# Both FFN up projections as seven half-size products: two weight sums per layer in HBM, two on VectorE

## The reference, cut to what matters

```python
# first layer
h = rms_norm(x, norm2_g)                       # 512 x 1024
gate, val = split(h @ w_up, 2)                 # w_up: 1024 x 5632; each result 512 x 2816
gate = silu(causal_depthwise_conv(gate, ffn_dw_w, ffn_dw_b))   # 3 taps over tokens
x = x + (gate * val) @ w_down                  # w_down: 2816 x 1024
# second layer: the same with w_gate_2 and w_up_2 (1024 x 2816 each), w_down_2, and a final norm
```

## Time and profile before

| | us |
|---|---|
| median of three executions | 1204.06 |
| profiled execution, its own time | 1203.35 |
| span of the profile | 1201.5 |
| TensorE busy | 1169.1 (97%) |
| VectorE busy | 688.9 (57%) |
| ScalarE busy | 560.1 (47%) |
| GpSimd busy | 531.6 (44%) |

### The profile page before, as it was taken

The page is one execution under the profiler, slowest core; times in us unless marked ns, Lnnn a source line. Parts: engine busy times, 40 slices in busy tenths (PEclk is TensorE's granted clock), DMA queues, the critical chain, the costliest instruction groups (busy, mean ns, idle before and its releaser), DMA issues.

```text
span 1201.5 us, 17233 instructions
## 1 busy us (share of the span) xinstructions
PE 1169.1 (97%) x6948; PEld 976.3 (81%) x6948; DVE 688.9 (57%) x979; ACT 560.1 (47%) x881; POOL 531.6 (44%) x288
## 2 busy tenths in 40 slices
PE   7999999999999998999999999999899999999997
PEld 6877768788888886888877767778799999998886
DVE  5999973343332334444574577865956666674444
ACT  6356575333232323232445565655566665652323
POOL 3540033655545454445684220008445555564443
PEclk9999999999999998999989999999999999999999
DMA  5422021268978968867823120213255555642321
GB/s 181 140 78 96 4 70 35 71 231 226 236 242 207 243 234 209 201 243 203 207 57 113 64 71 28 80 37 106 70 169 182 182 187 178 191 162 83 105 89 70
DMA packets 115672, 167.75 MB, mean 140 GB/s; under 512 B 3363, under 2 KB 95882, under 8 KB 115594
## 3 DMA queue, kind: packets, MB, share of 16 engines
q1 hardware_dynamic: 102634, 120.26, 30.2%
q0 software_dynamic: 12800, 46.14, 16.0%
q10 hardware_dynamic: 160, 0.26, 0.1%
HBM read 164.29 MB, written 48.23 MB: 177 GB/s over the span
## 4 chain that ended last, share of the span: by engine, by line
PE 88%; DVE 5%; ACT 3%; issue 1%; POOL 1%; DMA 1%; POOLq 0%; ACTq 0%; DVEq 0%; SPq 0%
PE ps L2294 16%; PE ps L1960 13%; PE ps L1962 13%; PE ps L1961 13%; PE ps L2351 10%; PE ps L2355 10%; PE ps L2049 4%; PE ps L2539 3%; PE ps L2095 1%; DVE act_t L1508 1%; PE ps L2491 1%; PE ps L2080 1%; ACT w_hi L744 1%; PE ps L2410 1%; PE ps L2446 1%
## 5 line engine op out<-in xcount | busy, mean ns | idle before, releaser
L610 POOL TENSOR_TENSOR w_lo<-w_raw,w_hi 128x1024 fp32r<-128x1024 f32 x176 | 445.2, 2532 | 518.2 <-ACT w_hi L744 517.3
L744 ACT ACTIVATE w_hi<-w_raw 128x1024 fp32r<-128x1024 f32 x220 | 231.7, 1055 | 278.7 <-PE ps L1962 84.5
L1960 PE MATMUL ps<-h_hi,w_hi 128*128 128x512 f32 x656 | 261.7, 399 | 3.0 <-DVE h_lo L1347 2.1
L1961 PE MATMUL ps<-h_lo,w_hi 128*128 128x512 f32 x656 | 255.7, 390 | 0.0
L1962 PE MATMUL ps<-h_hi,w_lo 128*128 128x512 f32 x656 | 255.7, 390 | 0.0
L1558 DVE TENSOR_TENSOR tt<-act_t,tt 128x512 fp32r<-128x512 f32 x44 | 97.8, 2232 | 117.1 <-ACT tt L971 117.1
L1960 PEld LDWEIGHTS ps<-h_hi,w_hi 128*128 128x128 f32 x656 | 123.1, 188 | 36.3 <-issue 7.5
L1962 PEld LDWEIGHTS ps<-h_hi,w_lo 128*128 128x128 f32 x656 | 123.1, 188 | 26.2
L1961 PEld LDWEIGHTS ps<-h_lo,w_hi 128*128 128x128 f32 x656 | 123.2, 188 | 24.5 <-issue 0.5
L1565 DVE TENSOR_TENSOR ps<-ps,rbs 128x512 f32<-128x512 f32 x88 | 61.5, 698 | 120.2 <-PE ps L1962 118.9
L2294 PE MATMUL ps<-tt,w_hi 128*128 128x256 f32 x640 | 116.2, 283 | 0.0
(11 more groups left out here) (331 smaller groups left out, 1949.3 us busy)
## 6 DMA issues: line engine op xcount, KB each, us to landing
w_raw<-in_w_up SPq DMA_DIRECT2D x23, 1024.0 KB, 6.9
w_raw<-in_w_down SPq DMA_DIRECT2D x22, 1024.0 KB, 4.9
w_raw<-blocks SPq DMA_DIRECT2D x40, 512.0 KB, 3.6
w_raw<-in_w_in SPq DMA_DIRECT2D x19, 1024.0 KB, 5.1
blocks<-in_w_up POOLq DMA_DIRECT2D x12, 1408.0 KB, 10.5
blocks<-in_w_gate POOLq DMA_DIRECT2D x12, 1408.0 KB, 6.3
blocks<-blocks POOLq DMA_DIRECT2D x8, 1408.0 KB, 10.4
w_raw<-in_w_gate SPq DMA_DIRECT2D x20, 512.0 KB, 3.6
```

The source lines that it names most:

```text
L610: pool.tensor_tensor(unit_view(w_lo, at, flat), unit_raw(at, flat), unit_view(w_hi, at, flat).bitcast(F32), ALU.subtract).then_inc(s_lo, 1)
L744: act.activation(unit_view(w_hi, at, flat), unit_raw(at, flat), ACT.Copy).then_inc(s_hi, 1)
L1960: pe.matmul(ps[:, bank, :], whi, hi, start=first, stop=False, skip_group_check=True)
L1961: pe.matmul(ps[:, bank, :], whi, lo, start=False, stop=False, skip_group_check=True)
```

## The change

`NC` becomes `(1, 1)`: in both layers the first group stays plain and ten are blocks of seven products. Per layer only two weight sums are made in HBM, with 16 DMAs of the same size: S1 (unit of product 0) and S2 (unit of product 6). The first layer's 16 are issued by GpSimd during the first layer's in projection and attention (four among its units, eight in a row after unit 15, four in the out projection), the second layer's 16 during the first layer's up and down projection, one per block. The two other sums (units of products 3 and 4) are made by VectorE: S1 + A11 and then (S1 + A11) + A12, from the blocks of products 0, 1 and 2 that are loaded anyway, into a new buffer `sum_raw` of two units. So a block loads five units, not seven. A load may only overwrite a block after VectorE has used it (`s_sum`).

In the first block of a layer the products run in the order 1, 2, 0, 3, 4, 5, 6. The activations times the norm's gain are now written out once (`xg`, eight ScalarE instructions of 128x512 per layer), and the four activation sums are one VectorE instruction each of 128x1024, all after the norm's `spread`. The low parts of the activation sums move into the first group and first block. In the last block the first two `split_hi` and `split_lo` come earlier, and the down projection starts with banks 0 to 5 of its first two units before banks 6 and 7. The first four units of the down projection are loaded one by one. The cut diff:

```diff
-NC = (11, 1)
+NC = (1, 1)
 def on_vector(u):
-    return block_of(u) is not None and block_of(u)[1] in (1, 3, 5)
+    at = block_of(u)
+    return at is not None and at[1] in (1, 3, 5) and at not in ((0, 1), (NS[0], 1))
+SUMS_AFTER = {u: 1 for u in range(U_IN + 7, U_IN + 15, 2)}
+SUMS_AFTER[U_IN + 15] = 8
+SUMS_AFTER |= {u: 1 for u in range(U_OUT + 1, U_OUT + 8, 2)}
+SUMS_AFTER |= {u: 1 for u in range(U_UP + 4 * NC[0], U_DOWN, NB)}
+SUMS_AFTER |= {u: 1 for u in range(U_DOWN, U_DOWN + KF, 4)}
+FIRST_ORDER = (1, 2, 0, 3, 4, 5, 6)
+        sum_raw = sb("sum_raw", [P, 2, DM])
...
+            def one_block(u, src):                     # SP
+                before = LOADED[n - 4]
+                wait_lo(sp, before)
...
+                if block_of(before) is not None:
+                    if j < 3:
+                        sp.wait_ge(s_sum, 2 * g + (2 if j == 2 else 1))
...
                 for i in range(NC[lay], NUP):          # SP, up
-                    for j, src in enumerate((blocks[0, :, n], gate[0, 0:DK, n], gate[0, DK:DM, n], blocks[1, :, n],
-                                             blocks[3, :, n], val[0, DK:DM, v], blocks[2, :, n])):
-                        one_block(u + j, src)
+                    halves = {0: sums[0, :, n], 1: gate[0, 0:DK, n], 2: gate[0, DK:DM, n],
+                              5: val[0, DK:DM, v], 6: sums[1, :, n]}
+                    for at, j in enumerate(product_order(i, lay)):
+                        if j in halves:
+                            one_block(u + at, halves[j])
...
+            def half_sum(i, n):                        # VectorE
+                s1, a11, a12 = (u + order.index(j) for j in range(3))
+                if n == 0:
+                    wait_raw(dve, s1)
+                    wait_raw(dve, a11)
+                    if i > NC[lay]:
+                        wait_lo(dve, u - NB + 3)
+                    dve.tensor_tensor(unit_raw(u + 3, True), unit_raw(s1, True), unit_raw(a11, True), ALU.add)
+                else:
+                    dve.wait_ge(s_sum, 2 * g + 1)
+                    wait_raw(dve, a12)
+                    if i > NC[lay]:
+                        wait_lo(dve, u - NB + 4)
+                    dve.tensor_tensor(unit_raw(u + 4, True), unit_raw(u + 3, True), unit_raw(a12, True), ALU.add)
                 def quad(i):                           # VectorE
-                    if i == NC[lay] - 1 and NS[lay]:
-                        rest(u0 + 4 * NC[lay] + 1)
+                    if i == 0:
+                        half_sum(NC[lay], 0)
+                        half_sum(NC[lay], 1)
+                        cross_lo(lay, 1)
                 def sevenfold(i):                      # VectorE
+                    if first:
+                        cross_lo(lay, 2)
                     rest(u + 3)
+                    if not last:
+                        half_sum(i + 1, 0)
+                    rest(u + 5)
                     for c in range(2):
                         joined(c, 2, q1c, q1_at, left, CROSS)
-                    rest(u + 5)
+                    if not last:
+                        half_sum(i + 1, 1)
+                    if first:
+                        cross_lo(lay, 3)
+                        cross_lo(lay, 4)
...
+                    if j == 5:                         # TensorE, ready()
+                        if first:
+                            pe.wait_ge(s_tl, crossed + 3)
...
-                for k in range(KF - 2):                # TensorE, down
-                    ktile(u0 + k, k, first=(k == 0))
+                for ms in (range(6), range(6, KD)):
+                    for k in range(2):
+                        ktile(u0 + k, k, ms, first=(k == 0))
+                for k in range(2, KF - 2):
+                    ktile(u0 + k, k, range(KD))
```

More of the change, by code:

```diff
@@ L79, with in_first_down, is_sum @@
 LO_COUNT, USED_COUNT = unit_counts()
+def in_first_down(u):
+    return any(u0 <= u < u0 + 4 for u0 in (U_DOWN, U_DOWN2))
+def is_sum(u):
+    at = block_of(u)
+    return at is not None and at[1] in (3, 4)
+LOADED = [u for u in range(U_END) if not is_sum(u)]
+LOAD_AT = {u: n for n, u in enumerate(LOADED)}
 def raw_counts():
     pairs, firsts = [0, 0], [0, 0]
-    at = []
-    for u in range(U_END):
-        slot = (u // 2) % 2
-        alone = u < 4 or block_of(u) is not None
-        if u % 2 == 0 and alone:
+    at = {}
+    for n, u in enumerate(LOADED):
+        slot = (n // 2) % 2
+        alone = u < 4 or block_of(u) is not None or in_first_down(u)
+        if n % 2 == 0 and alone:
             firsts[slot] += 16
-            at.append((True, slot, firsts[slot]))
+            at[u] = (True, slot, firsts[slot])
         else:
-            if u % 2 == 0 or alone:
+            if n % 2 == 0 or alone:
                 pairs[slot] += 16
-            at.append((False, slot, pairs[slot]))
+            at[u] = (False, slot, pairs[slot])
     return at
@@ L674, in _ @@
             rests(U_UP + 3, 1)
-            for n, u in enumerate(range(U_UP + 4, U_IN2)):
-                rests(u, 1)
-                if n % 2 == 0 and n < 16 * PIECES:
-                    block_sums(n // 2)
-            rests(U_IN2, 2)
-            block_sums(8 * PIECES - 1)
+            rests(U_UP + 4, U_IN2 + 2 - U_UP - 4)
             for m in range(1, KD):
@@ L1643, in sevenfold @@
                         gated(1)
-                        for k in range(1, 4):
-                            split_lo(lay, k)
+                        split_lo(lay, 2)
+                        split_lo(lay, 3)
                     else:
@@ L2296, in product, with ready @@
                     mm.then_inc(s_q, 1)
-                wait_lo(pe, u)
-                if first:
-                    pe.wait_ge(s_tl, crossed + 1)
-                for c in range(2):
-                    if first:
+                def ready(j, c):
+                    if j == 0 and first:
+                        pe.wait_ge(s_tl, crossed + 1)
                         pe.wait_ge(s_gv, tiles + c - 1)
-                    else:
+                    elif j == 0:
                         pe.wait_ge(s_c, 8 * (g - 1) + 2 + c + 1)
-                    product(0, c)
@@ L2307, in sevenfold @@
-                wait_lo(pe, u + 1)
-                for c in range(2):
-                    if first:
+                    if j == 1 and first:
                         pe.wait_ge(s_conv, tiles + c - 1)
-                    else:
+                    elif j == 1:
                         pe.wait_ge(s_c, 8 * (g - 1) + 4 + 2 * c + 2)
-                    product(1, c)
-                wait_lo(pe, u + 2)
-                for c in range(2):
-                    if first and lay:
-                        pe.wait_ge(s_tc, 8)
-                    if not first:
-                        pe.wait_ge(s_c, 8 * (g - 1) + 4 + 2 * c + 1)
-                    product(2, c)
@@ L2334, in sevenfold @@
-                for c in range(2):
-                    pe.wait_ge(s_c, 8 * g + c + 1)
-                    product(5, c)
-                wait_lo(pe, u + 6)
-                for c in range(2):
-                    pe.wait_ge(s_qc, 8 * g + 4 + c + 1)
-                    product(6, c)
+                    if j == 2 and first:
+                        pe.wait_ge(s_rbs, lay + 1)
+                        if lay:
+                            pe.wait_ge(s_tc, 8)
+                    elif j == 2:
+                        pe.wait_ge(s_c, 8 * (g - 1) + 4 + 2 * c + 1)
@@ L2342, in down @@
+                for at, j in enumerate(product_order(i, lay)):
+                    wait_lo(pe, u + at)
+                    for c in range(2):
+                        ready(j, c)
+                        product(at, j, c)
             def down(lay, u0):
@@ L2357, in product, with ktile @@
                     return mm
-                def ktile(at, k, first=False):
+                def ktile(at, k, ms, first=False):
                     wait_lo(pe, at)
                     pe.wait_ge(s_alo, KF * lay + k + 1)
-                    for m in range(KD):
-                        if first and NS[lay]:
+                    for m in ms:
+                        if first:
                             done = 8 * (NS[0] * lay + NS[lay])
```

275 lines of the change are left out of this document (146 added, 129 removed).

## The result

The changed kernel takes 1239.2 us (median of four executions, 1238.08 to 1241.98) beside 1203.97 us for the kernel before on the same chip: a ratio of 1.0294, 95% interval 1.0275 to 1.0313. It is 3% slower, where 1201 us was forecast and the range ended at 1230. The profiled execution has a span of 1240.2 us, 38.7 more than the 1201.5 of before.

What follows compares the result with a forecast made beforehand. TensorE's matmuls were taken to bound the kernel (97% busy, 88% of the chain); 1203.35 - 16.0 + 15.1 + 8.0 - 8.0 - 1.8 = 1200.65, with 0.7 for the median 1201 us, range 1183 to 1230.

Steps and rivals of the forecast that it cites:

- term 2: Steady state of the new blocks, both layers: VectorE's loop exceeds TensorE's 20.16 us by 0.84, 18 transitions, +15.1 us.
- the rival: Blocks of both layers: GpSimd's low part of u+7 precedes the second half_sum, 2.4 us more per transition, 1244; chance 0.20.
- my sign for this rival: In the blocks: a unit's load taking over 3.7 us would show GpSimd's low part going ahead of the second half_sum.
- term 3: First block of each layer: waits for product 5, longer first transitions and delayed gate times val, together +8.0 us.
- The cover rival: Blocks of both layers: VectorE's slack holds, so the steady state costs zero and blocks take 20.16 us; 1184, chance 0.27.
- Term 1: First layer's up projection: ten plain groups of 21.76 us become blocks of 20.16 us, -16.0 us.
- Term 4: Ends of both up projections: holes and the slower clock behind the first mostly go, -8.0 us.
- Term 5: Ahead of the second layer's blocks: activation sums move behind the norm, ending TensorE's wait for h_lo, -1.8 us.
- Parts at nothing: First layer's 16 sum DMAs (eight in a row taking 57 us), xg copies and changed block loads: no cost.
- a small rival: First layer's blocks only: loads beside sum transfers take 4.4 us, lengthening the loop by 0.9; 1212, chance 0.09.

Runs made afterwards that it cites:

- e10: Changed kernel with VectorE's rest(u+5) swapped ahead of the first half_sum, so the A12 load is issued about 1.2 us earlier; 1206.55 us, ratio 1.0023.
- e13: Changed kernel with the second half_sum cut to 8 of its 1024 columns, its place and load wait kept; 1224.95 us, ratio 1.0187.
- e1: Changed kernel with the second half_sum adding A11 in place of A12, so it doesn't wait for the A12 load; 1214.56 us, ratio 1.0083.
- e7: Changed kernel with the second half_sum moved behind gated(0) of the same block; 1213.08 us, ratio 1.0078.
- e9: Changed kernel with the second half_sum moved behind gated(0) and ten sum transfers moved out of the first up projection; 1193.36 us, ratio 0.9917.
- e3: Changed kernel with rest(u+8) on VectorE moved between the taps, second half_sum unmoved; 1234.97 us, ratio 1.0261.

## Why the prediction was wrong, step by step

- **The step that failed is term 2, the steady state of the new blocks,** by its size. Forecast +15.1 us (18 transitions of 0.84). Measured by the block distances: 9 x (22.92 - 20.16) + 9 x (22.45 - 20.16) = +45.4. The mechanism was the one described, and in the second layer so were its two levels: the quiet transitions come at 20.9 to 21.1 us (21.0 forecast), most others at 23.3 (23.4 in the rival). What failed is the choice between them: I gave GpSimd's low part of u+7 ahead of the second sum 0.20 and "the load is alone in flight" as the reason against, with a margin of 0.2 us; it came in 8 of the 18 transitions. The load is not to blame: in the block shown it took the usual 3.6 us, so my sign for this rival, a load of over 3.7 us, did not show, and GpSimd was first all the same.
- **These eight don't explain all of it.** At the 2.4 us of the rival they are 19.2 us, which makes 34.3 of term 2. The other 11 lie mainly in the first transition of each layer (24.6 us, of which term 3 had only 1.4) and in the first layer's one of 28.1, whose load was held up beside a sum transfer. e10 moves the margin by 1.2 us and shortens the loop by as much, and gets 33 us back; e13 shows that it is GpSimd's turn and not the sum's length.
- **The slow clock had no term.** I named it only as something that a large hole may cost. In the trace after, TensorE's holes inside the blocks are 23.0 us in the first layer and 19.7 in the second, and the lower clock level cost half of 20.5 and of 10.2 us more, 15.4 in all. That is 58.0 us together, nearly the same as terms 2 and 3 by the other count (45.4 + 12.9).
- **The cover rival was wrong** for the order as written, but 20.2 us a block is there to be had: e1 and e7 reach it in the second layer, without the load wait and with the sum moved, and e9 in both layers.
- **Term 1 held** (-16.0), as far as e9 shows it: its first up projection is 11.6 us shorter than before with 20.22 us a block, and its holes at the start (6.2 us) take most of the rest. In the kernel after it is buried.
- **Term 3 was too small.** The first blocks' stalls alone are 2.0 + 0.5 + 5.1 in the first layer and 4.9 + 0.4 in the second, 12.9 us against a forecast of 2.6 + 1.8 + 0.8 = 5.2; what the first transitions add (2 x 1.4 in the forecast) is in term 2's figure. In the second layer `rest(u+5)` met GpSimd and took 3.43 us, the A12 load was issued that much later, and `cross_lo` 3 stood behind it until 901.88.
- **Term 4 right in kind:** the hole at the end of the first up projection is 1.8 us in place of 4.3 and no slow clock follows (504 down matmuls in 114.5 us, before 116.9), the second 1.1 in place of 2.7: about -6.5 of the -8.0. **Term 5** fits (the wait of 1.8 us for h_lo is gone; down projection to second norm: 371.6 to 365.8, of which 2.4 is the clock), though not resolved from the 1.6 us that are left in that stage.
- **"Parts at nothing" was wrong in this profiled execution:** attention ended 5.1 us late. The eight transfers in a row were issued from 90.6 to 157.2, 67 us in place of the 57 that I had summed. GpSimd's low parts still began on time (158.42), but the transfers behind them were pushed back: one was issued at 177.86 after GpSimd had waited 4.77 us for the one before, GpSimd's inverse root came at 178.5 in place of 175.5, TensorE waited 1.9 us for `diag`, and its clock stood at the lower level from 181.3 to 188.1, which costs 3.4. Seven of the ten runs above show 236.0 to 236.1, as before, and three 237.3 to 237.7, so it is not a steady cost (this execution took 1241.98 us, the median was 1239.2); why it varies was not tried.
- The sum by the measured terms is -16.0 + 45.4 + 12.9 - 6.5 - 1.8 + 5.1 = +39.1, against 38.7. That it is so close is partly luck: 1.6 us less in the stage of the down projection and 1.0 us more in the last stage are explained by none of them.
- **A cause that I had only as a small rival** (the first layer's loads beside the sum transfers, 1212) is real and was partly hidden: in the first up projection it is 22.5 us once the order is mended and 6.0 before.

## What to carry to other kernels

When an engine's instruction waits for a load and is queued ahead of others, look at what a second engine does at that moment: a margin of 0.2 us in such a loop is no margin. Here both outcomes were taken, in 8 and 10 of 18 transitions. Put a sum of loaded data as late as its reader allows, not as soon as its operand might be there. And undo suspected causes in pairs, and compare stage by stage: a cause that shows 2 us in the whole time can be worth 6 in its stage, and 20 when the other is gone.

## What the runs showed of the hardware

- An element-wise VectorE instruction on two SBUF operands of 8 columns lasts up to 2.37 us beside GpSimd's 2.40 us one; in the other order GpSimd's took 3.36. With one input in PSUM (`joined`, taps: 0.42, 0.75 us) nothing of this is seen: beside GpSimd's low parts they are as long as without.
- A single adding transfer of 1408 KB beside four loads of 512 KB stretches these from 3.6 to 11.6 us, with the DMA engines busy all the time (share 1.07, 265 GB/s in 324 to 332 us of e7).
- In the up projections of the kernel after the granted clock fell six times, each time during or within 0.8 us behind a hole of TensorE of 2.2 us or more, and came back after 3.4 or 6.8 us. Five other holes of 2.2 us were not followed by it, and in e3 none of its 1.5 us holes was.
- In e10 the distance of blocks settles on 18.8 and 22.2 us by turns instead of a steady 20.5: presumably a slow block gives the next one its operands early (argued, not tried). A mean block time over two transitions would have hidden the collision.
